# Mixer of a hybrid decoder layer: seven block products for the up-projection, the down-projection as its own stage

## The reference

```python
h2 = rms_norm(x, lp['norm_ffn'])
up = jnp.einsum('btd,df->btf', h2, lp['w_up'])                  # 1024 -> 2 * 3072
up_c, new_ffn_buf = causal_dwconv(up, ffn_buf, lp['ffn_conv_w'], lp['ffn_conv_b'])   # width 3
act = jax.nn.gelu(up_c[..., :D_FF]) * up_c[..., D_FF:]
x = x + jnp.einsum('btf,fd->btd', act, lp['w_down'])            # 3072 -> 1024
```

## Time and profile before

| | us |
|---|---|
| median of 3 runs (lowest, highest) | 1938.87 (1938.74, 1942.5) |
| span of the profiled execution | 1936.0 |
| TensorE busy in that span | 1887.3 |
| VectorE, ScalarE, GpSimd busy | 1278.9, 868.7, 43.7 |
| mixer, from its first matmul to the end | 1080.2 to 1936.0 |

### The profile page before, as it was taken

The page is one execution under the profiler, slowest core; times in us unless marked ns, Lnnn a source line. Parts: engine busy times, 40 slices in busy tenths (PEclk is TensorE's granted clock), DMA queues, the critical chain, the costliest instruction groups (busy, mean ns, idle before and its releaser), DMA issues. The chain is left out here.

```text
span 1936.0 us, 37599 instructions
## 1 busy us (share of the span) xinstructions
PE 1887.3 (97%) x13112; PEld 1712.6 (88%) x13112; DVE 1278.9 (66%) x2835; ACT 868.7 (45%) x1686; POOL 43.7 (2%) x78
## 2 busy tenths in 40 slices
PE   6999999999999999979999999999999999999998
PEld 6999999999999999956665999989898999999896
DVE  6776767676767676875544774748475665748476
ACT  6766657575757474743343431313031322314033
POOL 0000000000000000031100000000000000000000
PEclk9999999999999999989999999999999999999999
DMA  6421211111212122399994220202021111102012
GB/s 200 154 63 50 66 50 59 54 54 52 63 46 64 45 60 72 134 343 370 377 347 164 66 65 24 77 11 77 11 66 33 55 44 45 55 23 76 11 46 105
DMA packets 166409, 182.86 MB, mean 94 GB/s; under 512 B 9542, under 2 KB 138534, under 8 KB 166294
## 3 DMA queue, kind: packets, MB, share of 16 engines
q1 hardware_dynamic: 165081, 180.66, 28.3%
q10 hardware_dynamic: 1212, 0.81, 0.1%
HBM read 162.49 MB, written 24.20 MB: 96 GB/s over the span
## 5 line engine op out<-in xcount | busy, mean ns | idle before, releaser
L1298 PE MATMUL ps<-h_hi,w_hi 128*128 128x384 f32 (+1 forms) x1152 | 386.6, 336 | 5.0 <-DVEq L1013 3.4
L1298 PE MATMUL ps<-h_hi,w_lo 128*128 128x384 f32 (+1 forms) x1152 | 376.5, 327 | 0.0
L1298 PE MATMUL ps<-h_lo,w_hi 128*128 128x384 f32 (+1 forms) x1152 | 376.4, 327 | 0.0
L2432 PE MATMUL ps<-h_hi,f_w_hi 128*128 128x320 f32 (+1 forms) x1136 | 370.7, 326 | 0.8 <-PEq L1587 0.8
L2432 PE MATMUL ps<-h_hi,f_w_lo 128*128 128x320 f32 (+1 forms) x1136 | 370.4, 326 | 0.0
L2432 PE MATMUL ps<-h_lo,f_w_hi 128*128 128x320 f32 (+1 forms) x1136 | 370.2, 326 | 0.0
L2511 ACT ACTIVATE yc<-ps,f_prm 128x384 f32<-128x384 f32 x144 | 93.3, 653 | 556.6 <-PE ps L2432 382.8
L2412 PE MATMUL ps<-d_hi,act 128*128 128x512 f32 x816 | 257.1, 390 | 0.5 <-issue 0.5
L1298 PEld LDWEIGHTS ps<-h_hi,w_hi 128*128 128x128 f32 x1152 | 217.2, 189 | 9.0 <-issue 4.0
L1298 PEld LDWEIGHTS ps<-h_lo,w_hi 128*128 128x128 f32 x1152 | 217.1, 188 | 0.6
L1298 PEld LDWEIGHTS ps<-h_hi,w_lo 128*128 128x128 f32 x1152 | 216.8, 188 | 0.0
(11 more groups left out here) (320 smaller groups left out, 2894.0 us busy)
## 6 DMA issues: line engine op xcount, KB each, us to landing
k<-in_cache_k SPq DMA_DIRECT2D x64, 512.0 KB, 6.5
vr<-in_cache_v SPq DMA_DIRECT2D x60, 512.0 KB, 6.4
w_raw<-in_w_in SPq DMA_DIRECT2D x48, 512.0 KB, 3.9
f_raw<-in_w_up SPq DMA_DIRECT2D x48, 512.0 KB, 3.9
f_raw<-in_w_down SPq DMA_DIRECT2D x24, 512.0 KB, 3.7
bias<-bias_tiles_dram SPq DMA_DIRECT2D x8, 576.0 KB, 3.8
merged_dram<-mg SPq DMA_DIRECT2D x8, 544.0 KB, 2.7
wo_raw<-in_w_out SPq DMA_DIRECT2D x8, 512.0 KB, 5.8
```

The costliest lines, as they stand in the source:

```text
L1298: last_ = pe.matmul(bank(s)[:, 0:n], w[:, W_SLOT[g], k, :], x[:, k, off:off + n], start=(k == 0 and i == 0), stop=(k == KT - 1 and i == 2))
L2432: l_ = pe.matmul(ps[:, e % 6, 0:n], w[:, p, k, :], x[:, k, off:off + n], start=(k == 0 and i == 0), stop=(k == KT - 1 and i == 2))
```

## The change

The up-projection of a pair is done as a two-by-two block product: gate and value columns are the block rows, the two halves of the 1024 channels the inner blocks, and two halves of the tokens the block columns. Strassen's scheme in Winograd's form makes of it seven products of half the depth in place of eight. The tokens are cut in two pieces `p` of 2 x 256 and 2 x 288 columns (each half of piece 1 with 32 sampled tokens). On the token side the forms B11, B21, B22, T1 to T4 of each piece are built and split once, during the first pair, which runs piece by piece; on the weight side GpSimd builds S1 to S4 for every pair and takes their low parts and the value block's. Three products are copied out on the way by ScalarE (`snap`); VectorE sums the parts of C11, C22 and C12 (`parts`), and ScalarE copies the fourth (`corner`), into whole rows `U` of 1106 tokens, over which the conv's taps now run in single instructions. The activations go to DRAM (`act_dram`), 544 KB per pair.

The down-projection follows when all 24 pairs are done. It runs in three passes `g` over three token tiles each; a pass goes through all 24 blocks, sums in six banks, and loads and splits each block's weights and activations anew, in three slots. The residual is stored to DRAM (`x2_dram`) in the stage before and loaded again by GpSimd's queue at the end of each pass. The stage before no longer does the mixer's first matmuls; `low` is gone, `high` copies without splitting. The loop over pairs holds 21 of 24.

```diff
-            pe.wait_ge(f0_lo, 1)
-            pe.wait_ge(h2lo_done, 6)
-            first_unit(0, range(0, KT))
             turn(7)
-            pe.wait_ge(h2lo_done, 12)
-            first_unit(1, range(0, KT // 2))
             turn(8)
-            first_unit(1, range(KT // 2, KT))
...
+P1, P2, P6, P5, P7, P3, P4 = range(7)
+PRODUCTS = [("A11", "B11", "u", True), ("A12", "B21", "w", True), ("S2", "T2", "u", False), ("S1", "T1", "v", True),
+            ("S3", "T3", "u", False), ("S4", "B22", "v", False), ("A22", "T4", "u", False)]
+BANK = {"u": 0, "w": 2, "v": 4}
...
+DT = 3
+DGROUP_BANKS = [(2, 3, 6, 7, 0, 1), (4, 5, 2, 3, 6, 7), (0, 1, 4, 5, 2, 3)]
...
+            def load_value(n):
+                if not first(n - 1 if isinstance(n, int) else n):
+                    sp.wait_ge(lv_done, n)
+                    sp.sem_inc(settled, 1)
+                sp.dma_start(rV[:, :, :], c.w_up[:, :, bass.ds(128 * n + DFF, 128)]).then_inc(rv_in, 16)
...
+            def store_act(n):
+                sp.wait_ge(av_done, n + 1)
+                sp.sem_inc(settled, 1)
+                row = c.act_dram[bass.ds(n, 1), :, :].rearrange("a p n -> p (a n)")
+                sp.dma_start(row[:, 0:SEQ], Y[1][:, 0:SEQ]).then_inc(act_out, 16)
...
+            def load_down(g, it, r):
+                if not (g == 0 and isinstance(it, int) and it == 0):
+                    sp.wait_ge(dn_done, block_count(g, it, r) - DT)
+                if g == 0 and r == 0 and isinstance(it, int) and it == NP // DT - 1:
+                    sp.wait_ge(act_out, 32 * NP)
+                sp.sem_inc(settled, 1)
+                f = DT * it + r
+                sp.dma_start(d_raw[r][:, :], w_dn[:, bass.ds(f, 1), :].rearrange("p a n -> p (a n)"))\
+                  .then_inc(d_in[r], 16)
+                row = c.act_dram[bass.ds(f, 1), :, :].rearrange("a p n -> p (a n)")
+                if g < 2:
+                    sp.dma_start(a_raw[r][:, :], row[:, 384 * g:384 * (g + 1)]).then_inc(d_in[r], 16)
                 else:
+                    sp.dma_start(a_raw[r][:, NS:NS + 256], row[:, 768:SEQ]).then_inc(d_in[r], 16)
+                    sp.dma_start(a_raw[r][:, 0:NS], row[:, SEQ:NTOK]).then_inc(d_in[r], 16)
...
+            def body(n):
+                if not last_(n):
+                    load_gate(n + 1)
+                    load_value(n + 1)
+                if first(n):
+                    sp.wait_ge(ls_done, 4)
+                    sp.dma_start(fprm[:, :, :, :], c.fprm_dram.rearrange("p (a k r) -> p a k r", a=2, r=FROW))\
+                      .then_inc(prm_in, 16)
+                else:
+                    store_act(n - 1)
+                if last_(n):
+                    sp.wait_ge(up_done, upc(n, P2, 1))
+                    sp.wait_ge(act_out, 32 * (NP - 2))
+                    for r in range(DT):
+                        load_down(0, 0, r)
+                    sp.dma_start(gain[:, :], broadcast_row(ins["norm_final"], 128)).then_inc(g_in, 16)
+                if not first(n):
+                    store_states(sp, n - 1)
...
+            def low_sum(n, name):
+                pool.wait_ge(hs_done, 4 * n + SPLIT_AT[name])
+                at = S_SLOT[name]
+                pool.tensor_tensor(lS[:, at, :, :], sum_raw(n, name), hS[:, at, :, :].bitcast(F32), ALU.subtract)\
+                    .then_inc(ls_done, 1)
...
+            def sums(n):
+                pool.wait_ge(rg_in, 16 * n)
+                pool.wait_ge(rv_in, 16 * n)
+                s = {name: sT[:, S_SLOT[name], :, :] for name in S_SLOT}
+                pool.tensor_tensor(s["S1"], rV[:, 0:4, :], rV[:, 4:8, :], ALU.add).then_inc(sum_done, 1)
+                pool.tensor_tensor(s["S3"], rG[:, 0:4, :], rV[:, 0:4, :], ALU.subtract).then_inc(sum_done, 1)
+                pool.wait_ge(sum_done, 4 * (n - 1) + SUM_AT["S1"])
+                pool.tensor_tensor(s["S2"], s["S1"], rG[:, 0:4, :], ALU.subtract).then_inc(sum_done, 1)
+                pool.wait_ge(sum_done, 4 * (n - 1) + SUM_AT["S2"])
+                pool.tensor_tensor(s["S4"], rG[:, 4:8, :], s["S2"], ALU.subtract).then_inc(sum_done, 1)
...
+            def body(n):
+                if first(n):
+                    low_sum(n, "S2")
+                    low_sum(n, "S1")
+                    low_value(n)
+                    low_sum(n, "S3")
+                    low_sum(n, "S4")
+                    pool.tensor_tensor(raw["T1", 1][:, :, :], quarter_of(ht, "B12", 1), quarter_of(ht, "B11", 1),
+                                       ALU.subtract).then_inc(tb_done, 1)
...
+                if not last_(n):
+                    sums(n + 1)
+                    for name in ("S2", "S1", "S3", "S4"):
+                        low_sum(n + 1, name)
...
+            def product(n, i, p):
+                a, b, bank, begins = PRODUCTS[i]
+                if first(n):
+                    if (b, p) != ("B11", 0):
+                        pe.wait_ge(tlo_done, LOW.index((b, p)) + 1)
+                elif i == P1:
+                    pe.wait_ge(la_done, n)
+                    pe.wait_ge(c21_done, 2 * (n - 1) + p + 1)
+                elif i == P2:
+                    pe.wait_ge(c_done, cnt(n - 1, C11, p))
+                elif i == P5:
+                    pe.wait_ge(c_done, cnt(n - 1, C12, p))
+                if a in SPLIT_AT:
+                    pe.wait_ge(ls_done, 4 * n + SPLIT_AT[a])
+                if i == P6:
+                    pe.wait_ge(snap_done, cnt(n, SNAP1, p))
...
+                if i == P4:
+                    pe.wait_ge(c_done, cnt(n, C22, p))
+                    pe.wait_ge(lv_done, n + 1)
+                wh, wl = weights_of(n, a)
+                xh, xl = hi[b, p], lo[b, p]
+                for k in range(4):
+                    for j, (w, x) in enumerate(((wh, xh), (wh, xl), (wl, xh))):
+                        l_ = pe.matmul(ps[:, BANK[bank] + p, 0:PN[p]], w[:, k, :], x[:, k, :],
+                                       start=(begins and k == 0 and j == 0), stop=(k == 3 and j == 2),
+                                       skip_group_check=not begins)
+                l_.then_inc(up_done, 1)
...
+            def body(n):
+                if first(n):
+                    for p in range(2):
+                        for i in range(7):
+                            product(n, i, p)
+                else:
+                    for i in range(7):
+                        for p in range(2):
+                            product(n, i, p)
+                        if i == P5:
+                            if third(n):
+                                pe.wait_ge(str_done, n - 1)
+                            turn_states(n - 1, 6)
...
+            def down(g, it):
+                if g == 2 and isinstance(it, int) and it == NP // DT - 1:
+                    for q in range(3):
                         for hf in range(2):
+                            for r in range(DT):
+                                if q == 0 and hf == 0:
+                                    pe.wait_ge(dlo_done, block_count(g, it, r))
+                                    pe.wait_ge(alo_done, block_count(g, it, r))
+                                l_ = rows(g, q, hf, r, False, r == DT - 1)
+                            l_.then_inc(td_done, 1)
+                        if q == 1:
+                            pe.wait_ge(add_done, 14)
...
+                    return
+                for r in range(DT):
+                    pe.wait_ge(dlo_done, block_count(g, it, r))
+                    pe.wait_ge(alo_done, block_count(g, it, r))
+                    begins = isinstance(it, int) and it == 0 and r == 0
+                    for q in range(3):
+                        for hf in range(2):
+                            if begins:
+                                bank_wait(g, q, hf)
+                            l_ = rows(g, q, hf, r, begins, end_of(g, it, r))
+                            if end_of(g, it, r) and (q, hf) != (2, 1):
+                                l_.then_inc(td_done, 1)
+                    l_.then_inc(dn_done, 1)
+                if g == 0 and isinstance(it, int) and it == 0:
+                    pe.wait_ge(c_done, 6 * NP)
+                    turn_states(NP - 1, 4)
...
+            def high_down(g, it, r):
+                if g < 2:
+                    act.wait_ge(d_in[r], 32 * (NP // DT * g + it + 1))
+                else:
+                    act.wait_ge(d_in[r], 32 * NP // DT * 2 + 48 * (it + 1))
+                if not (g == 0 and isinstance(it, int) and it == 0):
+                    act.wait_ge(dn_done, block_count(g, it, r) - DT)
+                act.activation(d_hi[r][:, :], d_raw[r][:, :], ACT.Copy).then_inc(dhi_done, 1)
+                if g < 2:
+                    l_ = act.activation(a_slot[r][:, 0:384], a_raw[r][:, :], ACT.Copy)
+                else:
...
+                l_.then_inc(ahi_done, 1)
...
+            def body(n):
...
+                snap(n, SNAP1, 0)
+                high_value(n)
+                snap(n, SNAP1, 1)
```

(86 more changed lines are left out.)

1023 lines of the change are left out of this document (573 added, 450 removed).

## The result

The changed kernel takes **1950.47 us** (median of 6 runs, 1947.26 to 1951.44) against 1940.76 for the kernel before in the same rounds: a ratio of 1.0047, 95% interval 1.0035 to 1.0059. That is slower by about half a per cent, by more than the 0.2% that can be told apart. The forecast was 1939.4 with a range of 1926 to 1957: the range holds the time, "slower" was the likeliest of the three signs, and the time itself is 11 us too low. The profiled execution has a span of 1947.8 us where my sum has 1936.5.

What follows compares the result with a forecast made beforehand. TensorE, 97% busy, was taken to bound the kernel. Start 1074.9, first pair 46.4, other pairs 493.8, down stage 314.0 and end 7.4 made a 1936.5 us span; plus 2.9, 1939.4 us, range 1926 to 1957.

Steps and rivals of the forecast that it cites:

- slower: Sign for the whole kernel: measurably slower than before, chance 0.43, against 0.29 for faster and 0.28 for the same.
- The gain of seven products: Up-projection: a pair's products take 21.20 us in place of 23.68, a gain of 59.4 us over 24 pairs.
- The term for fourteen waits: Up stage, each of the other 23 pairs: 0.15 us added to the pair for TensorE's waits.
- The corner chain: Between pairs: 2.45 us against 3.03 of cover, slack 0.6; as slower rival, it ends last: 1949, chance 0.10.
- my list: Per-pair work in the up stage: VectorE and GpSimd work that excludes each other fills 18.5 of 21.2 us.
- The start: End of the stage before: filling matmuls go, last norm and transposes decide; mixer begins at 1074.9 in place of 1080.2.
- The first pair: Up stage: forms are built while TensorE uses them, VectorE and GpSimd block each other; 46.4 us in place of 21.2.
- The down stage: Down-projection: 283.2 us of matmuls plus stalls at start, pass changes, third pass and last blocks, fold and transpose: 314.0 us.
- The slot loop of 7.85 us: Down stage: refilling a slot, with a 4.45 us landing, against 8.17 us of cover, 7.26 in the third pass.
- Rival 2: Down stage: feed longer than its cover, with a landing of 5.2 us; +13, 1952 us, chance 0.25.
- The base case: Whole kernel: the summed terms hold, 1939.4 us, own range 1932 to 1947, chance 0.40.
- Case 4: Faster: first pair -6, clock holds through stalls -4, loads land in 3.8 us; 1925 to 1931, chance 0.25.

Runs made afterwards that it cites:

- e10_forms_dve: Changed kernel with sums later, new start order, last blocks one by one, additions between low halves, four slots, first-pair differences on VectorE: 1901.92 us, ratio 0.9812.
- e1_sums_later: Changed kernel with GpSimd's four first-pair weight sums held until VectorE has made the sampled rows' low half: ratio 1.0019 to the kernel before.

## Why the prediction was right or wrong

- **The gain of seven products: right.** 84 products of each width at 119.5 and 132.9 ns make 21.20 us; the beat is 21.29, of which 0.11 is the transpose. The pitches from the rows hold to 0.1%. The term for fourteen waits (0.15; its own row, 0.35 us for 18 waits, would have made it 0.27) is nothing, since the products never wait; with it, 23 pairs came out 4.1 us too long. The corner chain that I gave 0.10 doesn't end last: no idle time in any beat, and 0.56 us only with 2 us of matmuls taken out. The room of the whole is smaller than my list said (18.5 of 21.2): the loop through GpSimd closes at 19.8.
- **The start: wrong, +8.0 us, and the worst miss.** The step that failed is that I counted the filling work and the queue at the end of the stage before, but not GpSimd's four new sums there. I had the row for it and used it for the first pair only. 4.0 us of it are VectorE's lengthened instructions. 2.6 are the clock: the 24 matmuls from 1060.30 on take 7.9 us where they took 5.3 before, and with the sums moved still 6.9 (e1_sums_later). 1.8 is the part of the trace before (the addition on which I compare comes at 1049.88 before and at 1051.66 after), which scatters between executions. That makes 8.4 of 8.0. With the sums moved and the clock up (e10_forms_dve) the stretch from the addition to the mixer is 24.7 us, and the forecast had 25.0, so nothing else was missing in it. The stores of residual rows, which I held to be harmless or 3 us, are harmless: that kernel has them too.
- **The first pair: mechanism right, size 3.1 us too big** (46.4 against 43.3). VectorE's instructions take 2.3 to 3.7 us, as forecast, and with GpSimd's differences gone the pair takes 34.1 us (523.8 less 23 x 21.29), against my lower bound of 28.3 without any blocking. I let the two engines exclude each other over the whole stretch; VectorE gets in free where GpSimd waits for a high half (1.23 us at 1088.67).
- **The down stage: +9.9 us.** The floor is 285.1 (283.2 + 2.0 in my sum). What each place costs can be read from the changed kernel's own matmuls, as the time between two starts above the 0.227 us of an even row; it takes in the wait, the refill behind it and the clock. Start 8.8 (forecast 6.4); pass changes 2.6 and 4.2, together 6.8 (6.7); last three blocks 8.2 (9); second pass 3.9 and third pass 10.4. With the rows' trip left out these last two are 0.2 and 4.5, for which I had 2 and 4.2. The step that failed is that the sum has no term for the trip: it costs 9.6 us in these two passes. The whole stage shows 7.8 between the two kernels, mostly because without the trip the clock fell behind the first pass change too (4.2 in place of 2.6). The trip isn't in the sum because I read "landing" as a property of a transfer and not of what else is under way; the traffic on GpSimd's queue stood in the change.
- **The slot loop of 7.85 us against a cover of 8.17** was right as a narrow margin: in the first pass the stage runs at 0.2267 us a matmul without stalls, and a landing of 8 us breaks it. Rival 2, "feed longer than cover", decided at 8.17; its time of 1952 came near, but not by an even 0.45 us in every loop: by few loads that land 4 us late. So the range held the time partly by luck: the likeliest sign was forecast for a loop that is too long throughout and for a corner chain, and neither came. The base case, with the miss at the start, would have been 1947.
- **The range and the chances.** Case 4, the fast one, came out in one part of three: the first pair did gain 3 us, the clock and the landings did not.

What is not settled: 0.7 us of the down stage, lost in steps too small to be told apart; and why the clock falls behind some waits and not behind others of the same length, as behind the 1.88 us ahead of the last output tile or the 2.35 and 2.33 at the first pass change.
